# The head of a transformer layer on one core: x loaded first, modulation columns made directly by TensorE, 16 identity transposes before the first product

## What is computed

```python
mod = silu(c) @ w_ada + b_ada                 # (6 * 1024)
sh_m, sc_m, g_m, sh_f, sc_f, g_f = split(mod, 6)
u = layer_norm(x) * (1 + sc_m) + sh_m
z = u @ w_in                                  # pool, q, k, v, conv, gates
...                                           # three mixer branches, merge, w_o
x = layer_norm(ALPHA * x + g_m * mix_out) * ln_mix_g + ln_mix_b
...                                           # squared-ReLU MLP, layer norm
```

## Time and profile before

| | us |
|---|---|
| median of 3 runs | 1428.12 (1427.02 to 1428.88) |
| the profiled execution | 1426.88 |
| its span in the trace | 1425.1 |
| TensorE busy (matmuls) | 1393.0, 98% of the span |
| VectorE busy | 969.4, 68% |
| ScalarE busy | 647.3, 45% |
| GpSimd busy | 421.8, 30% |

### The profile page before, as it was taken

The page is one execution under the profiler, slowest core; times in us unless marked ns, Lnnn a source line. Parts: engine busy times, 40 slices in busy tenths (PEclk is TensorE's granted clock), DMA queues, the critical chain, the costliest instruction groups (busy, mean ns, idle before and its releaser), DMA issues.

```text
span 1425.1 us, 17299 instructions
## 1 busy us (share of the span) xinstructions
PE 1393.0 (98%) x6522; PEld 1148.6 (81%) x6522; DVE 969.4 (68%) x1340; ACT 647.3 (45%) x914; POOL 421.8 (30%) x453
## 2 busy tenths in 40 slices
PE   7799999999999999999999999999999999999996
PEld 3688888888888888888888888888888888888885
DVE  5789677776479946464768797556565646437787
ACT  5522677777542124101616774443345535343251
POOL 1006465555566000000024327333444200001315
PEclk9899999999999999999999999999999999999998
DMA  9775465654565232762622555444445878456361
GB/s 347 266 266 159 148 185 156 188 168 149 161 234 172 89 104 79 245 192 86 200 114 89 183 181 193 142 145 146 156 163 207 297 277 299 162 211 236 118 222 60
DMA packets 159083, 256.42 MB, mean 180 GB/s; under 512 B 11352, under 2 KB 81422, under 8 KB 159000
## 3 DMA queue, kind: packets, MB, share of 16 engines
q1 hardware_dynamic: 144152, 204.97, 43.1%
q0 software_dynamic: 14848, 50.34, 10.5%
HBM read 182.36 MB, written 68.71 MB: 176 GB/s over the span
## 4 chain that ended last, share of the span: by engine, by line
PE 91%; DVE 5%; ACT 2%; issue 1%; DMA 1%; SPq 0%; DVEq 0%; ACTq 0%
PE ps L2065 24%; PE ps L2067 24%; PE ps L2066 24%; PE ps L2214 11%; PE ps L2254 2%; PE ps L2264 2%; PE ps L2279 2%; PE ps L2085 1%; DVE part_lo L1922 1%; PE ps L2129 1%; PE ps L2404 1%; DVE q L1983 0%; DMA k_raw<-tw_scratch 0%; DMA ada<-in_w_ada_dram 0%; DVE w_lo L1387 0%
## 5 line engine op out<-in xcount | busy, mean ns | idle before, releaser
L2065 PE MATMUL ps<-act_hi,w_hi 128*128 128x512 f32 (+1 forms) x480 | 187.2, 390 | 9.4 <-DVE act_lo L1482 9.4
L1922 DVE TENSOR_TENSOR part_lo<-k_raw,part_hi 128x1024 fp32r<-128x1024 f32 x112 | 146.1, 1332 | 58.6 <-ACT part_hi L935 55.4
L2067 PE MATMUL ps<-act_hi,w_lo 128*128 128x512 f32 (+1 forms) x480 | 184.6, 385 | 0.0
L2066 PE MATMUL ps<-act_lo,w_hi 128*128 128x512 f32 (+1 forms) x480 | 184.6, 385 | 0.0
L2065 PE MATMUL ps<-part_hi 128*128 128x512 f32 x448 | 174.3, 389 | 0.0
L2066 PE MATMUL ps<-part_lo,part_hi 128*128 128x512 f32 x448 | 174.3, 389 | 0.0
L2067 PE MATMUL ps<-part_hi,part_lo 128*128 128x512 f32 x448 | 174.3, 389 | 0.0
L935 ACT ACTIVATE part_hi<-k_raw 128x1024 fp32r<-128x1024 f32 x112 | 116.4, 1059 | 113.6 <-DMA k_raw<-tw_scratch 48.8
L2065 PEld LDWEIGHTS ps<-act_hi,w_hi 128*128 128x128 f32 x480 | 91.1, 190 | 28.4 <-issue 5.9
L1387 DVE TENSOR_TENSOR w_lo<-w_raw,w_hi 128x1024 fp32r<-128x1024 f32 x51 | 65.9, 1291 | 65.6 <-ACT w_hi L935 65.6
L2066 PEld LDWEIGHTS ps<-act_lo,w_hi 128*128 128x128 f32 x480 | 91.2, 190 | 18.4 <-issue 1.0
(11 more groups left out here) (260 smaller groups left out, 3202.4 us busy)
## 6 DMA issues: line engine op xcount, KB each, us to landing
k_raw<-h_scratch SPq DMA_DIRECT2D x112, 256.0 KB, 4.2
w_raw<-in_w_in_dram SPq DMA_DIRECT2D x42, 512.0 KB, 4.1
ada<-in_w_ada_dram SPq DMA_DIRECT2D x8, 2048.0 KB, 9.6
tw_rows<-in_w_ff_dram POOLq DMA_DIRECT2D x64, 256.0 KB, 4.1
tw_scratch<-tw_sum POOLq DMA_DIRECT2D x32, 512.0 KB, 3.7
h_scratch<-h_sum POOLq DMA_DIRECT2D x64, 256.0 KB, 3.0
k_raw<-tw_scratch SPq DMA_DIRECT2D x64, 256.0 KB, 5.4
pair_raw<-in_w_ff_dram SPq DMA_DIRECT2D x13, 1024.0 KB, 6.3
```

The source lines that it names most:

```text
L1922: nc.vector.tensor_tensor(part_lo[s][:, :, :], k_raw[rs][:, :, :], f(part_hi[s][:, :, :]), ALU.subtract)\
L2065: nc.tensor.matmul(out, sh, mh, start=first, stop=False)
L2066: nc.tensor.matmul(out, sh, ml, start=False, stop=False)
L2067: return nc.tensor.matmul(out, sl, mh, start=False, stop=last)
```

## The change

- SyncE's queue loads all of x first, then chunk 0, the small rows, chunk 2, blocks 0 and 1, chunk 1, block 2, chunk 3.
- Chunks 0 and 2 and the first half of chunk 3 are made by `direct_chunk`: 128 columns of `ada` are stationary, one column of silu(c) moves, and the output is a column of modulation values at once. One half chunk is 16 matmuls. The row, its copy and `row_columns` go. Each half of a chunk has its own column in PSUM, and `mixer_columns` adds the two.
- VectorE does only the second half of chunk 3.
- TensorE transposes tiles 0 to 5 of x before anything else; ScalarE works tile by tile instead of in pairs; VectorE copies tiles 6 and 7.
- 16 transposes of the identity into PSUM bank 0, whose result nobody reads, stand before the first product.

```diff
@@ SyncE
             def load_ada(i):
-                if i == 3:
-                    sp.wait_ge(head_ps_done, 1)
+                if i in (3, 5):
+                    sp.wait_ge(reduced, DIRECT_ORDER.index(i - 3) + 1)
                 elif i == 4:
                     sp.wait_ge(partial_done, 1)
-                elif i == 5:
-                    sp.wait_ge(head_ps_done, 4)
                 elif i == 6:
-                    sp.wait_ge(partial_done, 2)
+                    sp.wait_ge(reduced, 4)
...
-            load_ada_half(0, 0)
-            load_x(range(2))
-            load_ada_half(0, 1)
-            load_x(range(2, 4))
+            load_x(range(ST))
+            load_ada(0)
...
-            load_ada_half(2, 0)
-            load_x(range(4, 6))
-            load_ada_half(2, 1)
-            load_x(range(6, ST))
+            load_ada(2)
             load_block(0)
+            load_block(1)
             load_ada(1)
-            load_block(1)
+            load_block(2)
             load_ada(3)
-            load_block(2)
@@ ScalarE
-            for i in range(0, ST, 2):
+            for i in range(ST):
                 take_root(i, i)
-                take_root(i + 1, i + 1)
-                norm(i, i, mid[:, i, :])
-                if i + 1 < ST - 1:
-                    norm(i + 1, i + 1, mid[:, i + 1, :])
-                if i == 2:
-                    save_ada_row(0)
-                if i == ST - 2:
-                    save_ada_row(2)
-                    cut_hi(0)
-                    save_tile(i)
-                else:
-                    save_tile(i)
-                    save_tile(i + 1)
+                if i >= 1:
+                    norm(i - 1, i - 1, mid[:, i - 1, :])
+                if i >= 2:
+                    save_tile(i - 2)
+            cut_hi(0)
@@ VectorE
             def mixer_columns(h):
...
-                link(nc.vector.tensor_tensor(out, total, bias, ALU.add))
+                link(nc.vector.tensor_tensor(out, low, bias, ALU.add))
                 scale = mod[:, KT + 4 * h:KT + 4 * h + 4]
+                if h == 0:
+                    link(nc.vector.tensor_tensor(out, high, out, ALU.add))
+                else:
+                    link(nc.vector.tensor_tensor(scale, ps[:, 7, 28:32], scale, ALU.add))
...
             mixer_columns(0)
-            dve.wait_ge(z_done, ST)
-            nc.vector.tensor_copy(x_t[:, :, (ST - 1) * P:ST * P], tile_banks(ST - 1)).then_inc(x_copied, 1)
             cut_lo(0)
...
@@ TensorE
-            def row_chunk(i, half):
-
-                pe.wait_ge((ada_in, ada_end_in)[half][i % 3], 16)
-                for k in range(4 * half, 4 * half + 4):
-                    ins = nc.tensor.matmul(ps[0:1, ADA_BANKS[i], :], c_act[:, k:k + 1], ada[i % 3][:, k, :],
-                                           start=k == 0, stop=k == 7)
+            def direct_chunk(i, half):
+
+                pe.wait_ge((ada_in, ada_end_in)[half][i % 3], 16 * (i // 3 + 1))
+                if i == 3:
+                    pe.wait_ge(cols_done, 1)
+                for m in range(4):
+                    for k in range(4 * half, 4 * half + 4):
+                        col = 16 * half + 4 * i + m
+                        ins = nc.tensor.matmul(ps[:, 6 + i % 2, col:col + 1], ada[i % 3][:, k, m * P:(m + 1) * P],
+                                               c_act[:, k:k + 1], start=k % 4 == 0, stop=k % 4 == 3)
                 return ins
...
+            for i in range(6):
+                transpose_x(i)
             pe.wait_ge(head_sb_done, 2)
-            row_chunk(0, 0)
-            transpose_x(0)
-            transpose_x(1)
-            row_chunk(0, 1).then_inc(head_ps_done, 1)
-            transpose_x(2)
-            transpose_x(3)
+            direct_chunk(0, 0)
+            transpose_x(6)
+            direct_chunk(0, 1).then_inc(reduced, 1)
+            transpose_x(7)
...
-            row_chunk(2, 0)
-            transpose_x(4)
-            row_columns(0)
-            transpose_x(5)
-            row_chunk(2, 1).then_inc(head_ps_done, 1)
-            transpose_x(6)
-            row_columns(2)
-            transpose_x(7)
+            direct_chunk(2, 0)
+            direct_chunk(2, 1).then_inc(reduced, 1)
...
+
+            for m in range(16):
+                nc.tensor.transpose(ps[:, 0, m % 4 * P:(m % 4 + 1) * P], ident[:, :], ident[:, :])
...
             for n in range(2):
                 for k in range(2, 4):
                     rows_part(n, k)
+            direct_chunk(3, 0)
             pe.wait_ge(w_lo_done, 3)
             for k in range(4):
                 rows_part(2, k)
-            row_columns(1)
-            row_columns(3)
+            reduce_first(1)
+            reduce_first(3)
```

More of the change, by code:

```diff
@@ L66 @@
 N_DIRECT = 2
-ROW_ORDER = (0, 2, 1, 3)
-ADA_BANKS = {0: 0, 2: 1}
+DIRECT_ORDER = (0, 2, 1, 3)
 P1_BANKS = (4, 2, 0, 6, 0, 2)
@@ L125, in trunk_layer @@
     h_pad = at("h_pad", [P, 2, PAD + SEQ], f32, X + 84 * KB)
-    ada_row = [h_pad[0:1, i // 2, PAD + i % 2 * HALF:PAD + (i % 2 + 1) * HALF] for i in range(4)]
     z_pool = mid[:, 0:2, :]
@@ L960, in _ @@
             nc.scalar.activation(c_sig[:, :], c_raw[:, :], ACT.Sigmoid).then_inc(head_sb_done, 1)
-            def save_ada_row(i):
-                act.wait_ge(head_ps_done, {0: 1, 2: 4}[i])
-                copy(ada_row[i], ps[0:1, ADA_BANKS[i], :]).then_inc(head_sb_done, 1)
             def save_tile(i):
@@ L1408, in _ @@
             dve.wait_ge(head_sb_done, 2)
[L1409 to L1419, removed]
+            for t in range(ST):
+                dve.wait_ge(x_in[t], 16)
+                stats(mid[:, t, :], t)
+                if t >= 1:
+                    scale_bias(t - 1, t - 1)
+            scale_bias(ST - 1, ST - 1)
             dve.wait_ge(norm_ready, ST)
@@ L1428, in start_chunk @@
             def start_chunk(i):
-                dve.wait_ge(ada_in[i % 3], 16 * (i // 3 + 1))
+                if i == 3:
+                    dve.wait_ge(ada_end_in[0], 32)
+                else:
+                    dve.wait_ge(ada_in[i % 3], 16 * (i // 3 + 1))
                 if i == 4:
@@ L1434, in start_chunk @@
                     dve.wait_ge(reduced, i - 3)
-                link(nc.vector.tensor_scalar(partial_of(i)[:, :], ada[i % 3][:, 0, :], c_act[:, 0:1], None, ALU.mult))
-                add_rows(i, range(1, 4))
+                k0 = 4 if i == 3 else 0
+                link(nc.vector.tensor_scalar(partial_of(i)[:, :], ada[i % 3][:, k0, :], c_act[:, k0:k0 + 1], None,
+                                             ALU.mult))
+                add_rows(i, range(k0 + 1, 4))
             def end_chunk(i):
-                if i in (1, 3):
-                    dve.wait_ge(ada_end_in[i % 3], 16 * (i // 3 + 1))
-                add_rows(i, range(4, 8))
+                if i == 1:
+                    dve.wait_ge(ada_end_in[1], 16)
+                add_rows(i, range(5 if i == 3 else 4, 8))
             def add_rows(i, ks):
@@ L1469, in mixer_columns @@
                 ks = slice(4 * h, 4 * h + 4)
-                out, total, bias = (t.rearrange("p (g k) -> p g k", g=2)[:, :, ks]
-                                    for t in (mod[:, 0:16], ps[:, 6 + h, 0:16], cols[:, 0:16]))
-                link(nc.vector.tensor_tensor(out, total, bias, ALU.add))
+                out, low, high, bias = (t.rearrange("p (g k) -> p g k", g=2)[:, :, ks] for t in (
+                    mod[:, 0:16], ps[:, 6 + h, 0:16], ps[:, 6 + h, 16:32], cols[:, 0:16]))
+                link(nc.vector.tensor_tensor(out, low, bias, ALU.add))
                 scale = mod[:, KT + 4 * h:KT + 4 * h + 4]
+                if h == 0:
+                    link(nc.vector.tensor_tensor(out, high, out, ALU.add))
+                else:
+                    link(nc.vector.tensor_tensor(scale, ps[:, 7, 28:32], scale, ALU.add))
                 nc.vector.tensor_scalar_add(scale, scale, 1.0).then_inc(mod_done, 1)
@@ L1483, in cut_u_lo @@
                     .then_inc(u_lo_done, 1)
+            for t in (ST - 2, ST - 1):
+                dve.wait_ge(z_done, t + 1)
+                dve.wait_ge(x_copied, ST - 2)
+                nc.vector.tensor_copy(x_t[:, :, t * P:(t + 1) * P], tile_banks(t)).then_inc(x_copied, 1)
+            dve.wait_ge(head_ps_done, 2)
+            nc.vector.tensor_copy(cols[:, 0:ROWS_A], ps[:, 7, PIECE:PIECE + ROWS_A])
+            nc.vector.tensor_copy(cols[:, ROWS_A:ROWS_A + ROWS_C], ps[:, 7, PIECE + P:PIECE + P + ROWS_C])\
+                .then_inc(cols_done, 1)
             mixer_columns(0)
-            dve.wait_ge(z_done, ST)
-            nc.vector.tensor_copy(x_t[:, :, (ST - 1) * P:ST * P], tile_banks(ST - 1)).then_inc(x_copied, 1)
             cut_lo(0)
@@ L1492, in _ @@
             cut_u_lo(2)
+            cut_u_lo(3)
             start_chunk(1)
-            cut_u_lo(3)
+            cut_lo(2)
             end_chunk(1)
-            cut_lo(2)
             ada_chunk(3)
@@ L2079, in _, with reduce_first @@
             pe.wait_ge(consts_done, 2)
```

(20 more changed lines are left out.)

## The result

The change makes the kernel slower: 1445.7 us as the median of four executions (1444.92 to 1448.94) against 1428.1 before, a ratio of 1.0128 with a 95% interval of 1.0111 to 1.0146. That is 17.6 us, twice what was forecast, and the profiled execution, the slowest of the four, shows 22.0 (span 1447.1 against 1425.1). The time went roughly where rival A had put it: the clock stood at half through most of the head.

The account below looks back on a forecast made before the run. TensorE's program order in the head was taken as the bound: first product 6.4 us later plus 2.2 more at the return, 8.6 on the profiled 1426.88, gives 1435.5; with 1.24 for the median, 1436.8. Range 1432.5 to 1451.

Parts of the forecast that it names:

- rival A: One-column matmuls leave TensorE at 1.2 GHz throughout the head: 21.8 us later, 1450 us; chance 0.20.
- Direction and place: Slower, through the head: first product 6.4 us later, return to channel tiles 4 to 7 another 2.2; slower had 0.90.
- The new order: Tiles 0 to 5 first in the head: tile 0 at 5.3 us, tile 5 transposed at 23.2, last column at 39.0.
- warm case: Clock full throughout the head: first product 4.0 to 4.2 us later, 6.2 us of delay in all, 1434.3 us.
- The price of a direct instruction: In the half chunks, one of 32 instructions takes 0.105 us at full clock, 0.20 at half.
- Rival B: Direct columns in the head and chunk 3 much cheaper, down to 0.03 us an instruction: 1422 us; chance 0.04.
- The clock in the head: TensorE enters the half chunks at half clock, which rises after 2.9 to 6.4 us: 2.4 us lost.
- three cases before: Earlier rises to full speed: 6.40 us at the start, 4.4 behind 39.14 us, 2.9 behind 64.58 us.
- Chunk 3's half: The half chunk of chunk 3 on TensorE adds 3.36 us in front of block 2, not hidden.
- The identity transposes: 16 in the wait before the first product, at no cost, probably keep the clock full: gain 0.6 us, at least 0.
- C: The clock rises and falls in the head: 11 to 18 us later, 1440 to 1446 us; chance 0.10.

Follow-up runs that it names:

- order_alone: The change's sequence kept, but chunks 0 and 2 made by rows and chunk 3 on VectorE: 1433.5 us, ratio 1.0041.
- change_again: The change unedited, run and profiled once more: 1447.8 us, ratio 1.0138.
- method_alone: The kernel before with direct columns for chunks 0 and 2 in the places of the rows, chunk 3 on VectorE: 1437.7 us, ratio 1.0072.
- chunk3_vector: The change with chunk 3 wholly on VectorE again, all else kept: 1442.9 us, ratio 1.0111.
- before_all_three: The kernel before with VectorE's order, 32 identity transposes before the first product and 28 in the second pause: 1424.8 us, ratio 0.9981.
- transposes_between: The change with 12 more identity transposes in each half chunk of chunks 0 and 2: 1455.7 us, ratio 1.0184.

## Why the prediction was wrong

- **Direction and place: right.** The bound was the two moments in the head, the first product and the return, and 21.4 of 22.0 us lie there.
- **The new order: right.** Tile 0 was there at 5.09 us (5.3 predicted), tile 5 transposed at 21.9 (23.2; ScalarE's step is 2.13 us, not 2.4). `order_alone` came out at 6.3 us; that the forecast's warm case has 6.2 is in part chance, since that one includes the half chunk of chunk 3 (3.36 us) and `order_alone` does not, while its first product came 5.6 us later instead of 4.0 to 4.2.
- **The price of a direct instruction: right at both clocks,** 0.108 against 0.105 and 0.207 to 0.215 against 0.20. Rival B, which needed 0.066, is out.
- **"The clock in the head": this step failed.** It took 2.4 us, on the thought that the clock is half when the half chunks begin and rises within 6.4 us as in three cases before. In the profiled execution it was the reverse: the transposes had raised it by 16.5 us, and the direct columns let it fall at 22.7. In `change_again` it was half at the start of the chunks, as thought. In neither did it rise under them: 29 and 33 us of continuous work brought nothing. The four half chunks took 26.1 us instead of 13.4 + 2.4, and two tiles 3.6 instead of 2.0. All three cases of a rise had 512 moving columns behind them; I carried them over to one moving column.
- **Chunk 3's half: right in size** (3.46), but the fall behind it was not forecast: some eight instructions of block 2 at 0.43 us instead of 0.23, some 1.6 us.
- **The identity transposes: open.** They cost nothing on the path. They were to find the clock full and keep it so; in both profiles of the change they ran at half and did not raise it. The gain was put at 0.6 us; the medians say 2 to 4, by intervals that overlap.
- **Rival A's mechanism is what happened** in the profiled execution, and the nearness of its number, 22.1 against 21.8, is in part luck. A puts the first product 19.0 us later and the return 2.8 behind that; measured were 17.0 and 4.4. It counts three tiles on the path where there are two (and the text on the order says two), so 3 us for what was 1.7, and it has no second fall. The median lies between it and the forecast, in C's place. Two of the three faster executions spend some 9 us less at the half clock, an estimate from their mean clock of 0.984 against 0.981; the third has 0.981 too, and none of the three was profiled. The mechanism of A had 0.20; it should have had more than the forecast, since no row showed the clock over a long run of such matmuls. The evidence that I set against it, a full clock over 1.69 us and after, covered an eighth of the stretch in question.
- **Two slips in the sums** change nothing: 6.2 us of delay is 1434.3, as the range has it, not 1434.5, and the delay of B leaves out the clock's 2.4 where it gives 0.066 and 0.048.

## What to carry to other kernels

Before work is changed to matmuls with one moving column, ask how long TensorE will do nothing else: priced at the full clock the method saved 2.7 us, at the clock that it got it cost 9 to 10. A busy TensorE is not a sign of a full clock, so read the granted clock over the stretch, and test a new shape by itself in its old place first. And when the slow clock and a wait for another engine share one stretch, removing either alone may show nothing, as here: look for the next wait and take them out together.

## What the runs showed of the hardware

- The clock falls while TensorE works without a pause, if the work is matmuls with 128 stationary and one moving column (full at 21.9 us, half from 22.7, `method_alone` at 20.6 and 27.5), and under them it stays at half (20.8 to 61.8 us in `change_again`, of which the chunks and tiles take until 53.8). With 512 moving columns on one stationary column the clock stayed full over the same stretch (21 to 45 us, `order_alone`). No run has a number of columns in between, so what it is in the shape that matters, the one moving column or the 128 columns loaded for it, is not shown. The Trainium skill, in "TensorE: Matmul & The Clock Gate", has busy work release the throttle (Part 1); the runs here show that this kind of work did not.
- Transposes can raise and hold it, but not in each execution: single tiles of x, all that TensorE had done, ran at 1.80 us for eight and then 1.09 from 16.5 us on, with pauses of 1 us between them, and 32 identity transposes held it through the wait before the first product. Against that, it fell among the same tiles in `change_again` and `chunk3_vector`, during 28 transposes in a row in `before_all_three` (60.8), and 12 transposes in each half chunk did not hold it (`transposes_between`). The Trainium skill, in the same page's Part 4 (PE-mode transpose), says that the full clock does not engage for them; the rise with transposes alone decides against it for plain f32 transposes, though it is no sure thing.
- One-column matmuls, each with its own weight load of 128 f32 columns, are 0.108 us apart at the full clock and 0.207 to 0.215 at the half. That the load sets this pace is argued, from the weight loads' being busy 13.7 of the 13.8 us of the 64 instructions. The Trainium skill, in the same page's section "LDWEIGHTS (loading the stationary operand)", has a formula that gives, as an estimate, 107 ns for 128 columns, and names no dependence on the clock; the spacing agrees with it at the full clock and is twice that at the half clock.
- The same kernel's executions differ by up to 5.4 us (eight of the change, 1444.9 to 1450.3), against 3.5 us for 33 executions of the kernel before on one chip (1426.0 to 1429.4). That the clock's moves within the head make the difference is likely but not shown.
